# Rebuilding the router stage of a decoder trunk: residual put into the accumulators by identity products, counts in fp32r, an unturned split h, gates computed behind the selection, a first gather over four banks

## The chip, the cores and the metric

One core of one Trainium2 chip runs the whole program. The metric is the device time of one execution in microseconds (us); a kernel is timed in several runs and the median is given. One execution is also recorded by the hardware profiler; its span, from the first to the last recorded instruction, is a little shorter than its device time.

The engines are called PE (TensorE; its weight loads are listed apart as PEld), DVE (VectorE), ACT (ScalarE), POOL (GpSimd) and SP (SyncE, which here only issues transfers).

## The reference, cut to what matters

One layer, 256 tokens, model width 1024, fp32. The change touches the last of its three parts only, the mixture of experts:

```python
x = x + grouped_moe(rms_norm(x, norm_ffn), router_w, router_b, w_gate, w_up, w_down)

logits = h @ router_w + router_b                # 16 experts in 4 groups of 4
probs = softmax(logits)
best = argmax(sum of the two largest of each group)
top_p, top_i = the two largest of that group    # two experts for each token
top_w = top_p / sum(top_p)
out = sum over e of gate_e * ((silu(h @ w_gate[e]) * (h @ w_up[e])) @ w_down[e])
```

Each expert has two matrices of 1024 by 512 and one of 512 by 1024, and all 16 are read from memory.

## The kernel before, in words

Each engine has an instruction stream written out by hand, and the streams meet at semaphores. Before the experts come the mixers and the cross-attention, in which fp32 products are made of fp32r halves (`hi` and `lo`); the change leaves them as they are. Each product is one or more passes on PE, and each pass loads its stationary operand (up to 128 columns, `LDWEIGHTS`) and streams the moving one. An fp32 product is two passes, an fp32r product and a transpose are one.

The output projection of the cross-attention (chunks `C_XO`, `C_XO + 1`) leaves x in `x_res` (128 partitions, two token tiles of 1024), its first 512 columns before its last 512. Then the router:

- PE turns x (L1394), ACT moves it out times a gain (`x2_out`, L756), and PE makes the router logits (`router_products`, L1716). DVE makes `h_full` = x times a gain row, in halves of 512 columns (`h_part`, L1201). ACT reorders it to `h_turn` so that each 128-column tile of h is contiguous (`h_turned`, L778) and rounds it to `h_hi` (L787); DVE makes `h_lo` = `h_turn` - `h_hi` (L1363).
- DVE ranks the experts in a chain of small instructions that ends in `chosen` (L1265), and goes on with the gates (L1266 to L1276). PE makes counts out of `chosen`: five fp32 products with matrices of ones and of a strict triangle (L1747 to L1751). DVE turns them into places (`posm`), the number of rounds and one-hot selections `sel` (`select_tile`, L1290), one instruction for each token tile.
- PE clears the four banks in which the experts' outputs gather by products with zeros (`clear_banks`, L1740): two banks before it waits for `chosen`, two behind the counts.
- `slot_gates` (L1762) brings the gates and the inverse norms of the tokens into slot order; `first_gather` (L1773) then gathers h for the first group of four experts, 8 tiles of 4 passes each. It has two banks: ACT empties the even tiles (L794), DVE the odd ones (L1330), and tile t waits for tile t - 2 to be moved.
- In `expert_round` PE goes through the 16 experts: `gate_up` (L1829, 32 passes of 512 columns), `turn_gate_up`, `down` (L1844, 16 passes), `scatter` (L1864). The gathers for the groups behind the first (24 tiles) stand between these, one bank each. `rounds`, read from memory into a register by every engine ahead of its loop, is 1 here or 2 to 4 for uneven routings; the recorded execution has one round.
- At the end DVE adds the four accumulator banks to `x_res` (L1385), 512 columns each, and SP sends each piece out as it is ready (L485).

SP loads the experts' weights, 96 blocks of 1 MB, into a ring of 16 buffers (`expert_load`, L459); block n waits until PE has used block n - 16 (`mm_done`).

Of the kernel before, what the change touches and what calls it, by code (L numbers as in the profile page):

```python
# [23 lines left out]
P = 128  # L24
S = 256
NT = S // P
D = 1024
# [68 lines left out]
def build_program(nc, d_in, out):  # L96
# [6 lines left out]
    with ctx:  # L103
# [123 lines left out]
        h_hi, h_lo = sb("h_hi", [P, NT, D], f32r), sb("h_lo", [P, NT, D], f32r)  # L227
        h_turn = at("h_turn", xg_at + 8192, [P, NT, D])
# [8 lines left out]
        y_hi, y_lo = sb("y_hi", [P, COLS], f32r), sb("y_lo", [P, COLS], f32r)  # L237
        route = sb("route", [P, 1024])
        router_w = sb("router_w", [P, KD, NE])
        g_ffn_row = sb("g_ffn_row", [P, D])  # L240
        zeros = sb("zeros", [P, P])[:]
# [8 lines left out]
        def sem(name):  # L250
# [32 lines left out]
            out_ready half_rsqrt_ready slot_gates_moved zeros_written x2_rows odd_moved""".split()  # L283
# [128 lines left out]
        def _(sp):  # L412
# [69 lines left out]
            for i in range(NT):  # L482
                for half in range(2):
                    sp.wait_ge(s["out_ready"], 2 * i + half + 1)
                    sp.dma_start(out[0, i * P:(i + 1) * P, half * COLS:(half + 1) * COLS],  # L485
                                 x_res[:, i, half * COLS:(half + 1) * COLS]).then_inc(ld["out"], 16)
# [4 lines left out]
        def _(act):  # L491
# [271 lines left out]

            for i in range(NT):
                x2_square(0, i)
            x2_out(0)
# [9 lines left out]
            def h_turned(n):  # L776
                half = slice(n * P // 2, (n + 1) * P // 2)
                A(h_turn[:].rearrange("q i (t p) -> q i t p", t=KD)[:, :, :, half],  # L778
                  h_full[:].rearrange("q i (p t) -> q i t p", t=KD)[:, :, :, half], ACT.Copy)
# [80 lines left out]
        def _(dve):  # L860
# [332 lines left out]
            V.memset(zeros, 0.0).then_inc(s["zeros_written"], 1)  # L1193
# [10 lines left out]
            h_part(0, 1).then_inc(s["h_full_done"], 1)  # L1204
            dve.wait_ge(mm_done, first_block[C_XO + 2])
# [59 lines left out]
            V.scalar_tensor_tensor(v84(chosen), v84(rank), 2.0, one_group, ALU.is_lt, ALU.mult).then_inc(s["chosen"], 1)  # L1265
            V.tensor_tensor(v84(topw), v84(r2), one_group, ALU.mult)  # L1266
            dve.drain()
            V.reduce_sum(rsum, v2(topw), AX.X)
            dve.drain()
            V.reciprocal(rrec, rsum)  # L1270
            dve.drain()
            V.tensor_tensor(v2(gates), v2(topw), two(rrec, NE), ALU.mult)
            dve.drain()
            V.tensor_copy(gates_split[:, :, 0], v2(gates))
            dve.drain()
            V.tensor_tensor(gates_split[:, :, 1], v2(gates), f32(gates_split[:, :, 0]), ALU.subtract)  # L1276

            dve.wait_ge(s["places_done"], 1)
            V.scalar_tensor_tensor(posm, ps[:, 1, 0:NT * NE], 1.0, chosen, ALU.add, ALU.mult)
# [22 lines left out]
            select_tile(1, slice(0, EPG)).then_inc(s["sel_ready"], 1)  # L1302

            def select(r, g):

                if g:
                    dve.wait_ge(s["sel_turned"], r * (2 * NG) + 2 * g)
                else:
                    dve.wait_ge(s["sel_turned"], r * (2 * NG))
                for i in range(NT):  # L1310
                    V.tensor_copy(gcur[:, i, :, 0:EPG], f32(gates_split[:, i, :, EPG * g:EPG * g + EPG]))
                    ins = select_tile(i, slice(EPG * g, EPG * g + EPG))
                ins.then_inc(s["sel_ready"], 1)
# [13 lines left out]
            def gather_out(r, g, t):  # L1327

                dve.wait_ge(s["gathered"], r * (NG * KD) + (KD * g + t + 1))
                V.tensor_copy(xg[g % 2][:, t].rearrange("p e c -> p (e c)"), ps[:, 1, 0:EPG * SLOTS]).then_inc(s["odd_moved"], 1)  # L1330
# [14 lines left out]
            def expert_round(r):  # L1345
                for e in range(NE):
                    g, j = e // EPG, e % EPG
                    more = g < NG - 1
                    if more and j >= 2:
                        for t in range(4 * j - 8, 4 * j - 4):  # L1350
                            gather_out(r, g + 1, t)
                    if more and j == 1:
                        select(r, g + 1)
# [15 lines left out]
            slot_gates(0, 0)  # L1369
            first_gather_out(0)  # L1370
            dve.wait_ge(s["rounds_ready"], 1)
            rounds = dve.value_load(n_rounds_i[0:1, 0:1], min_val=1, max_val=S // SLOTS)
            with dve.Fori(0, rounds) as r:
                with dve.If(r > 0):
# [3 lines left out]
                    slot_gates(r, 0)  # L1378
                    first_gather_out(r)
                expert_round(r)  # L1380
# [560 lines left out]
```

## Time and profile before

| | |
|---|---|
| device time, median of 3 runs | 626.14 us (624.36 to 628.16) |
| device time of the profiled execution | 624.99 us |
| its span | 623.2 us |
| PE busy | 600.1 us (96%), 2962 instructions |
| PE weight loads busy | 398.1 us (64%) |
| DVE, ACT busy | 275.0 us (44%), 238.0 us (38%) |
| bytes moved | 164.09 MB, mean 263 GB/s |

Busy is the time in which an engine has an instruction in work. Matmuls are pipelined, so a busy PE is not one at its peak: the spacing of the starts of its passes says more than their durations. A row of the timeline gives the start, the time from the first start to the last end, the instruction, and in brackets how long the engine was idle and what ended it.

### The profile page before, as it was taken

What the parts mean: (1) busy time and instruction counts of PE and PEld (TensorE: products, weight loads), DVE (VectorE), ACT (ScalarE), POOL (GpSimd) and SP (SyncE); (2) the same over time, 40 slices, a digit from 0 to 9 for tenths busy, and PEclk for the clock granted to TensorE, in tenths of its full rate; (3) what the DMA queues carried; (4) which work ended last, traced back from release to release, by engine and by line L of the source; (5) the groups of instructions that cost most, each with busy time, mean ns of one, the idle gap of its engine ahead of it and who ended that gap; (6) DMA issues with size and microseconds to landing.
All of it is one profiled execution on the core that took longest, in us unless ns stands there. A gap on an engine that the chain in (4) does not pass through costs nothing.

```text
span 623.2 us, 7542 instructions
## 1 busy us (share of the span) xinstructions
PE 600.1 (96%) x2962; PEld 398.1 (64%) x2962; DVE 275.0 (44%) x414; ACT 238.0 (38%) x318; POOL 19.1 (3%) x13
## 2 busy tenths in 40 slices
PE   4999999999999999999999998999999999999995
PEld 4887888877876777888888788434434434443332
DVE  3734686854577552887665646111102212110002
ACT  5643574654484544734544544311111111111111
POOL 0100000050020000000100100000000000000000
PEclk9999999999999999999999996999999999999999
DMA  9953566854552315756530599699999999999931
GB/s 331 371 204 137 178 228 212 294 202 136 161 155 89 102 69 209 223 176 202 168 103 1 197 426 420 268 418 423 420 421 421 421 421 422 421 420 420 423 155 67
DMA packets 49055, 164.09 MB, mean 263 GB/s; under 512 B 4377, under 2 KB 9179, under 8 KB 36732
## 3 DMA queue, kind: packets, MB, share of 16 engines
q1 hardware_dynamic: 44432, 158.81, 66.1%
q10 hardware_dynamic: 4588, 4.80, 2.4%
q8 instruction: 23, 0.38, 0.2%
q14 instruction: 12, 0.10, 0.0%
HBM read 162.53 MB, written 2.64 MB: 265 GB/s over the span
## 4 chain that ended last, share of the span: by engine, by line
PE 90%; ACT 3%; DVE 3%; issue 1%; DMA 1%; DVEq 1%; SPq 0%; POOL 0%; ACTq 0%
PE ps L1829 18%; PE ps L1421 15%; PE ps L1413 14%; PE ps L1414 14%; PE ps L1844 9%; PE ps L1394 5%; PE ps L1773 3%; PE ps L1864 3%; PE ps L1582 1%; PE ps L1557 1%; DMA w_raw<-in_w_in 1%; ACT w_hi L498 1%; PE ps L1693 1%; PE ps L1716 1%; PE ps L1740 1%
## 5 line engine op out<-in xcount | busy, mean ns | idle before, releaser
L868 DVE TENSOR_TENSOR w_lo<-w_raw,w_hi 128x2048 fp32r<-128x2048 f32 (+2 forms) x54 | 118.4, 2211 | 56.5 <-ACT w_hi L498 55.9
L1413 PE MATMUL ps<-w_hi,act_hi 128*128 128x512 f32 (+1 forms) x304 | 118.7, 392 | 1.8 <-ACT w_hi L498 1.8
L1414 PE MATMUL ps<-w_hi,act_lo 128*128 128x512 f32 (+1 forms) x304 | 116.3, 384 | 0.0
L498 ACT ACTIVATE w_hi<-w_raw 128x2048 fp32r<-128x2048 f32 (+2 forms) x54 | 99.1, 1856 | 26.9 <-PE ps L1421 26.1
L1829 PE MATMUL ps<-e_raw,xg 128*64 128x512 f32 x368 | 82.4, 596 | 0.0
L1421 PE MATMUL ps<-w_lo,act_hi 128*128 128x512 f32 (+1 forms) x304 | 74.2, 386 | 0.0
L1413 PEld LDWEIGHTS ps<-w_hi,act_hi 128*128 128x128 f32 x304 | 57.1, 188 | 14.3 <-issue 3.5
L1414 PEld LDWEIGHTS ps<-w_hi,act_lo 128*128 128x128 f32 x304 | 57.2, 188 | 10.6
L1421 PEld LDWEIGHTS ps<-w_lo,act_hi 128*128 128x128 f32 x304 | 55.6, 188 | 11.5 <-issue 0.7
L1829 PEld LDWEIGHTS ps<-e_raw,xg 128*64 128x64 f32 x368 | 25.1, 137 | 45.6 <-issue 44.0
L807 ACT ACTIVATE gu<-ps,rs_slot 128x512 f32<-128x512 f32 x16 | 11.0, 688 | 111.6 <-PE ps L1829 111.6
L1335 DVE SCALAR_TENSOR_TENSOR y_lo<-ps,w_slot,y_hi 128x512 fp32r<-128x512 f32 x16 | 12.0, 749 | 91.4 <-ACT y_hi L814 91.4
L1844 PE MATMUL ps<-e_raw,a_st 128*64 128x512 f32 x208 | 49.0, 601 | 0.0
L1330 DVE COPY xg<-ps 128x256 f32<-128x256 f32 x28 | 11.9, 425 | 72.9 <-PE ps L1773 72.9
L814 ACT ACTIVATE y_hi<-ps,w_slot 128x512 fp32r<-128x512 f32 x16 | 11.0, 688 | 68.5 <-PE ps L1844 68.5
L1829 PE MATMUL ps<-w_raw,xg 128*64 128x512 f32 x144 | 32.6, 597 | 1.1 <-DVE xg L1330 1.1
L845 POOL TENSOR_TENSOR stat<-stat,const 128x2 f32<-128x2 f32 (+2 forms) x9 | 18.9, 2100 | 353.7 <-DVE stat L895 176.0
L1844 PEld LDWEIGHTS ps<-e_raw,a_st 128*64 128x64 f32 x208 | 13.2, 136 | 23.2 <-issue 22.0
L1829 PEld LDWEIGHTS ps<-w_raw,xg 128*64 128x64 f32 x144 | 10.2, 136 | 18.1 <-issue 17.4
L1773 PEld LDWEIGHTS ps<-sel,h_hi 128*128 128x128 f32 x64 | 9.6, 188 | 19.0 <-issue 18.1
L1413 PE MATMUL ps<-w_hi,mg_hi 128*128 128x512 f32 x48 | 19.2, 400 | 0.0
L1414 PE MATMUL ps<-w_hi,mg_lo 128*128 128x512 f32 x48 | 19.0, 395 | 0.0
(299 smaller groups left out, 723.6 us busy)
## 6 DMA issues: line engine op xcount, KB each, us to landing
w_raw<-in_w_in SPq DMA_DIRECT2D x32, 1024.0 KB, 5.4
e_raw<-in_w_expert_down SPq DMA_DIRECT2D x26, 1024.0 KB, 14.8
e_raw<-in_w_expert_gate SPq DMA_DIRECT2D x23, 1024.0 KB, 14.2
e_raw<-in_w_expert_up SPq DMA_DIRECT2D x23, 1024.0 KB, 15.9
w_raw<-in_w_expert_gate SPq DMA_DIRECT2D x9, 1024.0 KB, 11.1
w_raw<-in_w_expert_up SPq DMA_DIRECT2D x9, 1024.0 KB, 13.5
w_raw<-in_w_expert_down SPq DMA_DIRECT2D x6, 1024.0 KB, 14.0
w_raw<-in_w_xkv SPq DMA_DIRECT2D x4, 1024.0 KB, 5.7
```

Source lines behind the costliest of these rows:

```text
L498: A(bview(w_hi, b, blocks[b].shape), bview(w_raw, b, blocks[b].shape), ACT.Copy).then_inc(hi_done, 1)
L845: nc.gpsimd.tensor_tensor(dst, src, minus_half[:, 0:w], ALU.pow).then_inc(s_rs[n], 1)
L868: V.tensor_tensor(bview(w_lo, b, sh), bview(w_raw, b, sh), f32(bview(w_hi, b, sh)), ALU.subtract).then_inc(lo_done, 1)
L1335: V.scalar_tensor_tensor(y_lo[:], ps[:, 3, :], w_slot[g % 2][:, j:j + 1], f32(y_hi[:]), ALU.mult, ALU.subtract).then_inc(s["y_lo_done"], 1)
L1394: return nc.tensor.transpose(dst, src, ident[0:n, 0:n])
L1413: MM(o, xh[:, t0 + k, i * P:(i + 1) * P], wh[:, k], start=first and k == 0, stop=False)
L1414: MM(o, xl[:, t0 + k, i * P:(i + 1) * P], wh[:, k], start=False, stop=False)
L1421: ins = MM(ps[:, banks + i, 0:width], xh[:, t0 + k, i * P:(i + 1) * P], wl[:, k], start=False, stop=last and k == nt - 1)
L1773: ins = MM(ps[:, bank, 0:EPG * SLOTS], hh[:, i, t * P:(t + 1) * P], sel[:, i, :, 0:SLOTS], start=not k and i == 0, stop=k == 1 and i == NT ...
L1829: ins = MM(ps[side(w), 0, :], xg[g % 2][:, 4 * half + t, j, :], raws[w][:, t * COLS:(t + 1) * COLS], start=half == 0 and t == 0, stop=half ...
L1844: ins = MM(ps[side(w), 3, :], a_st[:, 2 * half + f, :], raw[:, (2 * f + w) * COLS:(2 * f + w + 1) * COLS], start=half == 0 and f == 0, sto ...
L1864: ins = MM(ps[:, 4 + 2 * i + w, :], selT[side(w), j, i * P:(i + 1) * P], y[side(w), :], start=False, stop=False, skip_group_check=True)
```

## The change

- **Accumulators.** The zero products are gone. Instead PE puts x itself into the four banks by fp32 products of the identity with `x_res`, one of 512 columns for each bank: token tile 0 before it waits for `chosen`, tile 1 behind the counts. At the end the banks are only copied out, one half by ACT and one by DVE.
- **Counts.** `chosen` is written in fp32r, and so are the triangle and the ones (`count_w`). Four fp32r products take the place of five fp32 ones.
- **h.** `h_turn` is gone. `h_hi` and `h_lo` have the column order of `h_full` and are made in halves of 512 columns, the first ahead of the second half of x. The gathers read them with a step of 8 elements.
- **Gates.** The arithmetic on the gates stands behind the first gather on DVE, and `slot_gates` of the first group behind the first half of the first expert's gate/up products on PE.
- **Gather.** The first gather goes through banks 0 to 3, and tile t waits for tile t - 4.

```diff
@@ ACT
+            def h_hi_half(n):
+                cs = slice(n * COLS, (n + 1) * COLS)
+                act.wait_ge(s["h_full_done"], n + 1)
+                A(h_hi[:, :, cs], h_full[:, :, cs], ACT.Copy).then_inc(s["h_hi_done"], 1)
             for i in range(NT):
                 x2_square(0, i)
+            h_hi_half(0)
             x2_out(0)
...
             act.drain()
-            act.wait_ge(s["h_full_done"], 2)
-            h_turned(0)
+            h_hi_half(1)
             act.wait_ge(s["router_max_taken"], 1)
             A(prob[:], prob[:], ACT.Exp).then_inc(s["router_exp_done"], 1)
-            h_turned(1)
-            act.drain()
-            A(h_hi[:], h_turn[:], ACT.Copy).then_inc(s["h_hi_done"], 1)
...
-                    A(xg[0][:, t].rearrange("p e c -> p (e c)"), ps[:, 0, 0:EPG * SLOTS], ACT.Copy).then_inc(s["even_moved"], 1)
+                    A(xg[0][:, t].rearrange("p e c -> p (e c)"), ps[:, t % 4, 0:EPG * SLOTS], ACT.Copy).then_inc(s["even_moved"], 1)
...
+            for i in range(NT):
+                act.wait_ge(s["scattered"], rounds * (2 * NE) + i)
+                A(x_res[:, i, 0:COLS], ps[:, 4 + 2 * i, :], ACT.Copy).then_inc(s["out_by_act"], 1)
@@ DVE
             h_part(0, 1).then_inc(s["h_full_done"], 1)
+            def h_lo_half(n):
+                cs = slice(n * COLS, (n + 1) * COLS)
+                dve.wait_ge(s["h_hi_done"], n + 1)
+                V.tensor_tensor(h_lo[:, :, cs], h_full[:, :, cs], f32(h_hi[:, :, cs]), ALU.subtract).then_inc(s["h_lo_done"], 1)
+            h_lo_half(0)
...
-            V.scalar_tensor_tensor(v84(chosen), v84(rank), 2.0, one_group, ALU.is_lt, ALU.mult).then_inc(s["chosen"], 1)
-            V.tensor_tensor(v84(topw), v84(r2), one_group, ALU.mult)
...
+            V.scalar_tensor_tensor(v84(chosen_r[:].rearrange("p i e -> p (i e)")), v84(rank), 2.0, one_group, ALU.is_lt,
+                                   ALU.mult).then_inc(s["chosen"], 1)
+            h_lo_half(1)
...
-            for i in range(NT):
-                V.tensor_copy(gcur[:, i, :, 0:EPG], f32(gates_split[:, i, :, 0:EPG]))
+            select_tile(0, slice(0, EPG))
+            select_tile(1, slice(0, EPG)).then_inc(s["sel_ready"], 1)
             more_rounds(2)
             dve.drain()
-            select_tile(0, slice(0, EPG))
             more_rounds(3)
             dve.drain()
             V.tensor_copy(n_rounds_i[:], total[0:1, 1:2]).then_inc(s["rounds_ready"], 1)
-            select_tile(1, slice(0, EPG)).then_inc(s["sel_ready"], 1)
...
-            dve.wait_ge(s["h_hi_done"], 1)
-            for i in range(NT):
-                ins = V.tensor_tensor(h_lo[:, i, :], h_turn[:, i, :], f32(h_hi[:, i, :]), ALU.subtract)
-            ins.then_inc(s["h_lo_done"], 1)
-            slot_gates(0, 0)
             first_gather_out(0)
+            V.tensor_tensor(v84(topw), v84(r2), one_group, ALU.mult)
...
+            gates_of(0)
...
             for i in range(NT):
                 dve.wait_ge(s["scattered"], rounds * (2 * NE) + i)
-                for half in range(2):
-                    x_ = x_res[:, i, half * COLS:(half + 1) * COLS]
-                    V.tensor_tensor(x_, ps[:, 4 + 2 * i + half, :], x_, ALU.add).then_inc(s["out_ready"], 1)
+                V.tensor_copy(x_res[:, i, COLS:2 * COLS], ps[:, 5 + 2 * i, :]).then_inc(s["out_ready"], 1)
@@ PE
-            pe.wait_ge(s["zeros_written"], 1)
-            clear_banks(range(4, 6))
+            def residual(i):
+                for half in range(2):
+                    MM(ps[:, 4 + 2 * i + half, :], ident[:], x_res[:, i, half * COLS:(half + 1) * COLS], start=True, stop=False,
+                       skip_group_check=True)
+            residual(0)
...
             pe.wait_ge(s["chosen"], 1)
...
-            clear_banks(range(6, 8))
+            MM(ps[:, 1, 0:NT * NE], count_w[:, 0], chosen_r[:].rearrange("p i e -> p (i e)"), start=True, stop=False, skip_group_check=True)
+            MM(ps[:, 1, NE:2 * NE], count_w[:, 1], chosen_r[:, 0], start=False, stop=True, skip_group_check=True)
+            MM(ps[:, 1, 2 * NE:3 * NE], count_w[:, 1], chosen_r[:, 0], start=True, stop=False, skip_group_check=True)
+            MM(ps[:, 1, 2 * NE:3 * NE], count_w[:, 1], chosen_r[:, 1], start=False, stop=True,
+               skip_group_check=True).then_inc(s["places_done"], 1)
+            residual(1)
             pe.drain().then_inc(s["scattered"], 1)
...
             def slot_gates(r, g):
-                pe.wait_ge(s["sel_ready"], r * NG + (g + 1))
+                pe.wait_ge(s["sel_ready"], r * (2 * NG) + (2 * g + 2))
                 if g:
                     pe.wait_ge(s["selT_moved"], r * (2 * NG) + 2 * (g + 1) - 2)
+                else:
+                    pe.wait_ge(s["odd_moved"], r * ODD + 3)
...
-                        ins = MM(ps[:, bank, 0:EPG * SLOTS], hh[:, i, t * P:(t + 1) * P], sel[:, i, :, 0:SLOTS],
+                        ins = MM(ps[:, bank, 0:EPG * SLOTS], hh[:, i, t:D:KD], sel[:, i, :, 0:SLOTS],
...
             def first_gather(r, first=False):
+                pe.wait_ge(s["sel_ready"], r * (2 * NG) + 1)
                 for t in range(KD):
...
+                    if t >= 4:
+                        pe.wait_ge(s["odd_moved"], r * ODD + (t // 2 - 1)) if t % 2 else pe.wait_ge(
+                            s["even_moved"], r * (KD // 2) + (t // 2 - 1))
+                    gather_tile(0, t, t % 4, first)
...
                     gate_up(r, e, 0)
+                    if e == 0:
+                        slot_gates(r, 0)
...
-            slot_gates(0, 0)
             first_gather(0, first=True)
```

In `turn_selection` the first turn of a group now also waits for `slot_gates_moved`, and the first expert's gate/up products wait for three even tiles, and for the fourth only with their second half. For the groups behind the first, `gcur` is filled (`gates_of`) just ahead of the selection, as before, with a semaphore step of its own.

## Rows read from the trace of the kernel before

**Rows 1.** The granted PE clock on the page, 40 slices of the span, tenths of full
```profile
PEclk9999999999999999999999996999999999999999
```

**Rows 2.** PE's own waits from 393 to 617 us: total, times, longest
```profile
PE ps L1829 <- DVE xg L1330: 1.1, 1, 1.1
```

**Rows 3.** Windows: PE, PEld, DVE, ACT, POOL busy; granted clock; DMA share; GB/s
```profile
375.00:376.00 1.00, 1.00 (x9) 1.00 (x8) 0.56 (x4) 0.90 (x3) 0.00 (x0) 0.68 1.04 434
...
385.00:386.00 1.00, 0.92 (x7) 0.66 (x5) 1.00 (x2) 0.00 (x0) 0.00 (x0) 0.70 1.07 451
...
480.00:560.00 80.00, 80.00 (x402) 33.01 (x400) 13.75 (x34) 10.68 (x19) 0.00 (x0) 1.00 1.01 421
```

**Rows 4.** Timeline of DVE from the choice of experts to h_lo
```profile
379.10 0.19 DVE L1265 SCALAR_TENSOR_TENSOR route<-route 128x32 f32<-128x32 f32 x1
...
381.70 0.19 DVE L1279 SCALAR_TENSOR_TENSOR route<-ps,route 128x32 f32<-128x32 f32 x1 [0.66 <-PE ps L1751]
...
382.37 0.24 DVE L1295 CAST gcur<-gates_split 128x8 fp32r<-128x8 f32 x2
...
383.65 0.67 DVE L1290 TENSOR_TENSOR sel<-const,route 128x512 fp32r<-128x512 f32 x1
384.25 2.34 DVE L1363 TENSOR_TENSOR h_lo<-h_turn,h_hi 128x1024 fp32r<-128x1024 f32 x2
```

**Rows 5.** Timeline of PE: counts, cleared banks, slot gates
```profile
379.35 0.61 PE L1747 MATMUL ps<-route,const 128*128 128x16 f32 x2 [1.89 <-DVE route L1265]
...
381.08 0.59 PE L1751 MATMUL ps<-route,const 128*128 128x16 f32 x2
381.50 3.76 PE L1740 MATMUL ps<-zeros 128*128 128x128 f32 x16
385.35 1.16 PE L1762 MATMUL ps<-gcur,sel 128*128 128x10 f32 x8
```

**Rows 6.** Timeline of the first gather and the start of the first expert
```profile
386.36 0.49 PE L1773 MATMUL ps<-sel,h_hi 128*128 128x256 f32 x2
...
390.23 0.40 PE L1773 MATMUL ps<-sel,h_hi 128*128 128x256 f32 x2
390.46 0.40 PE L1773 MATMUL ps<-sel,h_lo 128*128 128x256 f32 x2
...
391.69 0.43 DVE L1330 COPY xg<-ps 128x256 f32<-128x256 f32 x1 [0.84 <-PE ps L1773]
...
392.76 7.09 PE L1829 MATMUL ps<-w_raw,xg 128*64 128x512 f32 x32 [1.11 <-DVE xg L1330]
```

**Rows 7.** Timeline of DVE and ACT around the first and last halves of h
```profile
364.30 1.29 DVE L1201 TENSOR_TENSOR h_full<-x_res,g_ffn_row 128x512 f32<-128x512 f32 x2
...
367.09 1.57 ACT L756 ACTIVATE x2T<-ps,vec_cols 128x256 f32<-128x256 f32 x4 [1.51 <-PE ps L1394]
...
369.39 1.29 DVE L1208 SCALAR_TENSOR_TENSOR x_res<-ps,x_res 128x512 f32<-128x512 f32 x2 [3.80 <-PE ps L1421]
...
377.88 1.91 ACT L787 ACTIVATE h_hi<-h_turn 128x2048 fp32r<-128x2048 f32 x1
```

**Rows 8.** Weight loads by form (busy, mean ns), then two bursts of transposes from the timeline
```profile
L1773 PEld LDWEIGHTS ps<-sel,h_hi 128*128 128x128 f32 x64 | 9.6, 188 | 19.0 <-issue 18.1 <-DVE xg L1330 0.7 <-DVE rs_slot L1325 0.2
...
L1394 PEld LDWEIGHTS ps<-ident,mem_x 128*128 128x128 f32 x16 | 1.9, 193 | 0.1
...
64.08 1.91 PE L1394 MATMUL ps<-ident,zq 128*128 128x128 f32 x16
...
261.58 1.95 PE L1394 MATMUL ps<-ident,mem_x 128*128 128x128 f32 x16
```

**Rows 9.** Timeline of the end
```profile
617.88 2.48 DVE L1385 TENSOR_TENSOR x_res<-ps,x_res 128x512 f32<-128x512 f32 x4 [0.83 <-PE ps L1864]
...
618.60 2.12 SPq L485 DMA_DIRECT2D out<-x_res  x4
```

**Rows 10.** The last four weight blocks, issues from 574 to 604 us, median us to landing
```profile
e_raw<-in_w_expert_down SPq DMA_DIRECT2D x4, 1024.0 KB, 20.3
```

More of the change, by code:

```diff
@@ L226, in build_program @@
         h_full = sb("h_full", [P, NT, D])
-        h_hi, h_lo = sb("h_hi", [P, NT, D], f32r), sb("h_lo", [P, NT, D], f32r)
-        h_turn = at("h_turn", xg_at + 8192, [P, NT, D])
+        h_hi = sb("h_hi", [P, NT, D], f32r)
         sel = sb("sel", [P, NT, EPG, P], f32r)
@@ L483, in _ @@
                 for half in range(2):
-                    sp.wait_ge(s["out_ready"], 2 * i + half + 1)
+                    sp.wait_ge(s["out_ready" if half else "out_by_act"], i + 1)
                     sp.dma_start(out[0, i * P:(i + 1) * P, half * COLS:(half + 1) * COLS],
@@ L1192, in _ @@
             act_lo_part("o", range(2), oT_lo, oT_hi)
-            V.memset(zeros, 0.0).then_inc(s["zeros_written"], 1)
+            V.tensor_copy(count_w[:, 0], before)
+            V.tensor_copy(count_w[:, 1], ones).then_inc(s["count_w_ready"], 1)
             residual_add(C_XO, 0, 1.0)
@@ L1264, in _ @@
             one_group = bc(first.unsqueeze(2), (P, NT * NG, EPG))
-            V.scalar_tensor_tensor(v84(chosen), v84(rank), 2.0, one_group, ALU.is_lt, ALU.mult).then_inc(s["chosen"], 1)
-            V.tensor_tensor(v84(topw), v84(r2), one_group, ALU.mult)
[L1267 to L1276, printed above, removed]
+            V.scalar_tensor_tensor(v84(chosen_r[:].rearrange("p i e -> p (i e)")), v84(rank), 2.0, one_group, ALU.is_lt,
+                                   ALU.mult).then_inc(s["chosen"], 1)
+            h_lo_half(1)
             dve.wait_ge(s["places_done"], 1)
-            V.scalar_tensor_tensor(posm, ps[:, 1, 0:NT * NE], 1.0, chosen, ALU.add, ALU.mult)
+            V.scalar_tensor_tensor(posm, ps[:, 1, 0:NT * NE], 1.0, f32(chosen_r[:].rearrange("p i e -> p (i e)")), ALU.add, ALU.mult)
             V.reduce_max(total[:, 0:1], ps[:, 1, NT * NE:NT * NE + NE], AX.X)
@@ L1301, in _, with gates_of @@
             V.tensor_copy(n_rounds_i[:], total[0:1, 1:2]).then_inc(s["rounds_ready"], 1)
-            select_tile(1, slice(0, EPG)).then_inc(s["sel_ready"], 1)
             def select(r, g):
[L1306 to L1309, printed above, removed]
+                dve.wait_ge(s["sel_turned"], r * (2 * NG) + 2 * g)
                 for i in range(NT):
-                    V.tensor_copy(gcur[:, i, :, 0:EPG], f32(gates_split[:, i, :, EPG * g:EPG * g + EPG]))
                     ins = select_tile(i, slice(EPG * g, EPG * g + EPG))
+                ins.then_inc(s["sel_ready"], 1)
+            def gates_of(g):
+                for i in range(NT):
+                    ins = V.tensor_copy(gcur[:, i, :, 0:EPG], f32(gates_split[:, i, :, EPG * g:EPG * g + EPG]))
                 ins.then_inc(s["sel_ready"], 1)
@@ L1329, in gather_out @@
                 dve.wait_ge(s["gathered"], r * (NG * KD) + (KD * g + t + 1))
-                V.tensor_copy(xg[g % 2][:, t].rearrange("p e c -> p (e c)"), ps[:, 1, 0:EPG * SLOTS]).then_inc(s["odd_moved"], 1)
+                bank = 1 if g else t % 4
+                V.tensor_copy(xg[g % 2][:, t].rearrange("p e c -> p (e c)"), ps[:, bank, 0:EPG * SLOTS]).then_inc(s["odd_moved"], 1)
             def y_lo_part(r, e):
@@ L1367, in first_gather_out @@
                     gather_out(r, 0, t)
-            slot_gates(0, 0)
             first_gather_out(0)
+            V.tensor_tensor(v84(topw), v84(r2), one_group, ALU.mult)
+            dve.drain()
+            V.reduce_sum(rsum, v2(topw), AX.X)
+            dve.drain()
+            V.reciprocal(rrec, rsum)
+            dve.drain()
+            V.tensor_tensor(v2(gates), v2(topw), two(rrec, NE), ALU.mult)
+            dve.drain()
+            V.tensor_copy(gates_split[:, :, 0], v2(gates))
+            dve.drain()
+            V.tensor_tensor(gates_split[:, :, 1], v2(gates), f32(gates_split[:, :, 0]), ALU.subtract)
+            dve.drain()
+            gates_of(0)
             dve.wait_ge(s["rounds_ready"], 1)
@@ L1799, in turn_selection @@
                     pe.wait_ge(s["selT_moved"], r * (2 * NG) + (2 * g + 1))
+                elif not half:
+                    pe.wait_ge(s["slot_gates_moved"], r * NG + (g + 1))
                 for e in (2 * half, 2 * half + 1):
@@ L1821, in gate_up @@
                     else:
-                        pe.wait_ge(s["even_moved"], r * (KD // 2) + KD // 2)
+                        pe.wait_ge(s["even_moved"], r * (KD // 2) + (4 if half else 3))
                         pe.wait_ge(s["odd_moved"], r * ODD + tiles // 2)
@@ L1873, in expert_round @@
                     gate_up(r, e, 0)
+                    if e == 0:
+                        slot_gates(r, 0)
                     if t0 is not None:
@@ L1914, in _ @@
                     pe.wait_ge(s["y_lo_done"], r * NE)
-                    slot_gates(r, 0)
                     first_gather(r)
```

32 lines of the change are left out of this document (7 added, 25 removed).

## The prediction, before the change was run

> **What bounds the kernel now.** I read the page's slices first: the granted PE clock is full in all 40 but the one from 374 to 389 us, the router [rows 1]. Then PE's waits behind the gather: one of 1.1 us, for the last tile of the first gather, and none for weights [rows 2]. Then the windows: from 480 to 560 us PE is busy in all 80.00 us, while the DMA engines are also full at 421 GB/s [rows 3]. So the experts are bound by PE, and what the change can win lies where PE stands still or runs slowly: between the choice of the experts and the first gate/up product, and behind the last product. The timelines of these two stretches are the basis of the sum. Everything behind the choice is one chain: it ends on DVE at 379.29, and the first gate/up pass starts at 392.76 [rows 4, 6]: 13.47 us. All else is a fixed load of PE that moves along with it.
>
> The clock in that stretch: in the slice of one us at 375 it was 0.68, and at 385 0.70 [rows 3]. As only 1.2 and 2.4 GHz occur, it fell at 375.36 and rose at 385.60, thus after 4.1 us of zero products and slot gates without a pause (from 381.50) [rows 5].
>
> **Ahead of the choice: nothing.** The first half of `h_full` is ready at 364.30 + 1.29 = 365.59. ACT has been free since 367.09 - 1.51 = 365.58 [rows 7]. `h_hi_half(0)` rounds 1024 elements; 2048 took 1.91 us [rows 7], so about 1.0: it ends near 366.65, 0.4 us ahead of the turned x that ACT takes next. `h_lo_half(0)` on DVE (1.2 us, half of L1363's two [rows 4]) ends near 367.9; behind it stands the residual sum, which starts at 369.39 at the call of PE [rows 7]. Both are covered; with ACT's cover of 0.4 us gone, x2 and the router's logits would be late by the excess. The second half of `h_hi` (1.0 us) takes the place of a reordering of 2.06 us, ahead of the Exp that DVE waits for. It may cost nothing; a gain is excluded, since the Exp waits for DVE's maximum.
>
> **Counts and places.** Before: ten passes from 379.35, the last starts at 381.08 + 0.22, and DVE begins at 381.70 [rows 4, 5]. Passes start every (381.08 - 379.35) / 8 = 0.216 us at the low clock, whatever their 16 columns. After: four passes, the last starts near 380.0 and ends near 380.4. DVE meanwhile does `h_lo_half(1)` from 379.25: 1.2 us, to 380.45. So `posm` starts at 380.45: **-1.25**. The fp32r form with 16 columns isn't in the trace; were each product still two passes, DVE would start at 381.25 (-0.45); it can't be before 380.45.
>
> **Selection.** Before, from 381.70 to the end of the second `sel` at 383.65 + 0.67 = 384.32: 2.62 us, of which 0.67 up to the casts at 382.37. After: 0.67, then two instructions of 0.69 (0.67 in the row): 2.05, so `sel` is ready at 382.50: **-0.57**. PE puts the second half of x into the banks meanwhile: 2 products, 4 passes of 512 columns, at 1.2 GHz 0.43 each, 380.2 to 381.9. That is hidden by 0.6 us; the passes before `chosen` stand where PE idled for 1.89 us [rows 5].
>
> **Slot gates.** Before, PE came out of the zero products at 385.35, a whole us behind `sel`, and began to gather at 386.36: 2.04 us from `sel` to gather. After: 0.05. The 8 slot gate passes come back behind the first half of the first gate/up: 1.01 us before [rows 5, 6], and a change of tile form besides, say 1.1. Net **-0.89**. The gates' chain on DVE lay between 379.29 and 381.70 [rows 4], so it takes 2.4 us at most, and 0.24 for the casts; from the last tile moved (388.3, below) it ends by 390.9. PE asks for it 3.5 us (16 of the 32 passes in 7.09 [rows 6]) behind the start of gate/up, at 392.3: hidden by 1.4 us. Behind PE's wait stand the second half of gate/up and the turns of `sel`; a chain later than that holds up all of PE.
>
> **Gather.** Before: 386.36 to 392.76, 6.40 us, at full clock almost throughout. Passes start every 0.115 to 0.12 us (390.23, 390.46: two of them), 32 would be 3.8; the rest was waiting for two banks to be emptied and 1.11 us from the last product to the first gate/up, while the copy ended at 392.12 [rows 6]. So 0.64 us of that last gap isn't the copy; it is the read of `rounds`, the entry into the loop, or both. With four banks PE doesn't wait for banks. But it starts at 382.55, when the clock is low. I take its rise at 385.4, near the 385.60 of the trace, since PE is at work again from about the same moment on; then 13 passes take 0.22 each, the other 19 0.119: 5.1, and 0.2 for the last to end: 387.85. The gap up to gate/up I take as 0.95, near the 1.11 seen and less only because the copy needn't be waited for; ends: 0.2 and 1.3. Gate/up starts at 388.8: 6.25 us, **-0.15**. The clock's ends: never low would give 382.55 + 3.8 + 0.2 + 0.95 = 387.5 (1.3 better); low to the end 32 x 0.22 = 7.0, gate/up at 390.75 (1.9 worse).
>
> **A step of 8 elements in the stationary operand,** 128 gather passes, 96 of them among the experts where PE has no slack. The trace has one operand with just this step, `mem_x`: 16 transposes in 1.95 us against 1.91 for contiguous `zq`, so 2.7 ns more for a pass, and its load 193 ns against the 188 that a contiguous gather load takes anyway [rows 8]. 128 x 2.7 ns: **+0.3**. Ends: 0 and 24 tiles x 0.07 (if each tile's first load lies bare) = 1.7.
>
> The Trainium skill (SBUF — State Buffer, the worked part on the DMA port swizzle) says that SBUF has 16-byte lines, and that every access that goes to a new line pays a penalty, so that fp32 is free only up to a step of 4. It gives no size, and the step of 32 bytes is beyond it; by the page the gather loads would lengthen, and the rows show 2.7 ns of it.
>
> **End.** Before, DVE's four sums end at 620.36 and SP issues from 618.60 to 620.72 [rows 9]. After, two pairs of copies of about 0.69 end near 618.6 and 619.3; SP needs about 0.4 for an issue, so it ends near 620.2. But 1 MB of output at the rate of [rows 3] takes 2.5 us from its start, so not all of it counts, and ACT may load a table behind its loop. **-0.3**; ends -0.7 and +0.3.
>
> **Sum:** -1.25 - 0.57 - 0.89 - 0.15 + 0.3 - 0.3 = -2.86. The profiled execution of 624.99 (span 623.2) would be 622.1, and on the median of the three runs, 626.14, the same 2.9 gives **623.2 us**. The loads of weights stay out of it: SP's issues come earlier with PE's first uses, and the DMA idled before 396, so it starts sooner by as much. The last four blocks land 20.3 us after their issue at 574.8 to 579 [rows 10], about 598, while PE uses them from 605 on.
>
> **Rivals.**
> 1. *The clock is hardly low* (or the loop's entry hides behind the gather). For: the identity products have 512 columns where the counts had 16, 1.7 us of them just before the gather. Against: in the trace the clock rose only 4.1 us into zero products of full load [rows 3, 5]. It gives -2.86 - 1.3 = -4.2, with the gap hidden -5.0: 621.1 to 622.
> 2. *The clock stays low through the gather.* For: PE has far less to do from 374.5 to 382.5 than before, 3 us of zero products are gone and those of 3.6 us halved. Against: the gather is as dense as the passes under which it rose. It gives -2.86 + 1.9 = -1.0: 625.2, and a low clock in gate/up besides would take the rest: 626.
> 3. *The stepped loads bind PE* (the other side). The price is paid 128 times; against the 3.2 us that the rest wins it decides from 25 ns a pass. Were the stepped read at half rate, a pass would take 0.218 instead of 0.109 (zq's spacing: 1.91 less the last pass's 0.27, over 15): 128 x 0.109 = +14, 637 us. For: no fp32r operand with a step stands in the trace, and a transpose's contiguous load is shorter than a product's, so `mem_x` may not tell of products. Against: its spacing, 2.7 ns. The page's rule above would be this rival at its full size.
> 4. *The chain isn't shortened at all,* because the gates on DVE or the slot gates hold up the first expert. It needs 1.4 us more than the rows give, and 4 to take the gain: 625 to 626.
>
> **How the numbers follow.** A difference of 0.5% (3.1 us) is about what a measurement of this kernel can tell from none. Chances: the sum as it stands, -1.6 to -4.0, 0.57; rival 1, 0.15; rival 2, 0.14; rival 3, 0.09 (half of it beyond +3.1); rival 4 and a late ACT or DVE ahead of the choice, 0.05. The likeliest is 3.1 us from the bound by a mere 0.2, so its 0.57 divides into 0.26 faster and 0.31 same. Faster: 0.26 + 0.15, and a little of the spread of the runs: 0.43. Slower: 0.045, 0.02, and the spread: 0.09. Same: 0.48. Range: from rival 1 at 620.8 to rival 2 with a cold gate/up and half of rival 4, 626.5.
>
> **What the profile after would show.** `posm`'s first instruction 1.3 us behind the choice instead of 2.4; the gather's first pass 3.3 us behind the choice instead of 7.1; starts of gather passes 0.22 apart, then 0.12 from about 385.5 on; the first gate/up 9.5 behind the choice; slot gates within gate/up without a wait; the loads of `h_hi` at 190 ns and gather tiles among the experts as long as before. I am wrong if those loads are well above 200 ns, if the clock is not back with the gather, or if the table load stands before ACT's last copies on the path.

## The result and the profile after

The changed kernel takes 637.08 us (median of 4 runs, 635.44 to 639.24), the kernel before 625.31 beside it: ratio 1.018, interval 1.014 to 1.021. It is slower by about 11.8 us, outside the range and on the side that the prediction gave 0.09. The profiled execution took 636.96 us, with a span of 635.2.

The page after, busy time and the clock (answers to [rows 1]):

```profile
PE 612.8 (96%) x2932; PEld 407.6 (64%) x2932; DVE 274.3 (43%) x413; ACT 235.3 (37%) x319; POOL 19.3 (3%) x13
...
PEclk9999999999999999999999998999999999999998
```

PE has 30 instructions fewer and is busy 12.7 us longer. The clock is not the reason: up to the last product it is low in one stretch of the router, as before, and for 6.8 us instead of 10.2. So PE has no more passes than before, and some take longer. The groups of weight loads show which (answers to [rows 8]: busy, mean ns):

```profile
L1781 PEld LDWEIGHTS ps<-sel,h_lo 128*128 128x128 f32 x64 | 18.6, 339 | 0.0
L1781 PEld LDWEIGHTS ps<-sel,h_hi 128*128 128x128 f32 x64 | 17.9, 328 | 19.9 <-issue 19.9
...
L1401 PEld LDWEIGHTS ps<-ident,mem_x 128*128 128x128 f32 x16 | 1.9, 193 | 0.1
```

The gather's loads went from 188 to 328 and 339 ns. The transposes of `mem_x`, which have the same step of 8 and on which the prediction priced it, are as they were. The timeline of PE around the second group's gather, among the experts, from the second expert's gate/up on:

```profile
401.29 7.09 PE L1837 MATMUL ps<-e_raw,xg 128*64 128x512 f32 x32
...
416.80 0.75 PE L1781 MATMUL ps<-sel,h_hi 128*128 128x256 f32 x2
417.39 0.64 PE L1781 MATMUL ps<-sel,h_lo 128*128 128x256 f32 x2
417.96 3.65 PE L1837 MATMUL ps<-e_raw,xg 128*64 128x512 f32 x16
```

The same in the kernel before:

```profile
401.31 7.09 PE L1829 MATMUL ps<-e_raw,xg 128*64 128x512 f32 x32
...
416.81 0.51 PE L1773 MATMUL ps<-sel,h_hi 128*128 128x256 f32 x2
...
417.49 3.65 PE L1829 MATMUL ps<-e_raw,xg 128*64 128x512 f32 x16
```

A tile (4 passes) takes 417.96 - 416.80 = 1.16 us from its start to the next work, and 417.49 - 416.81 = 0.68 before. There are 24 such tiles; added up over all of them in the two timelines it is 27.7 us against 15.7, so +12.0, or 0.125 us for each of their 96 passes.

Now the router. The timeline of DVE and PE from the choice of the experts to the first expert (answers to [rows 4, 5, 6]):

```profile
378.50 0.19 DVE L1272 SCALAR_TENSOR_TENSOR chosen_r<-route 128x32 fp32r<-128x32 f32 x1
378.61 1.22 DVE L1209 TENSOR_TENSOR h_lo<-h_full,h_hi 128x1024 fp32r<-128x1024 f32 x1
...
379.46 0.36 PE L1756 MATMUL ps<-chosen_r,count_w 128*128 128x16 f32 x1
379.68 3.76 PE L1746 MATMUL ps<-x_res,ident 128*128 128x512 f32 x4
379.86 0.19 DVE L1277 SCALAR_TENSOR_TENSOR route<-ps,chosen_r 128x32 f32<-128x32 f32 x1
...
380.53 1.29 DVE L1288 TENSOR_TENSOR sel<-const,route 128x512 fp32r<-128x512 f32 x2
...
383.67 0.82 PE L1781 MATMUL ps<-sel,h_hi 128*128 128x256 f32 x2 [0.23 <-issue]
...
391.60 3.65 PE L1837 MATMUL ps<-w_raw,xg 128*64 128x512 f32 x16
395.18 1.05 PE L1770 MATMUL ps<-gcur,sel 128*128 128x10 f32 x8
396.17 3.65 PE L1837 MATMUL ps<-w_raw,xg 128*64 128x512 f32 x16
```

The selection is ready at 380.53 + 1.29 = 381.82, but the gather starts at 383.67: PE is still at the identity products, whose four passes start 0.86 us apart and last to 383.44. The clock in that stretch (windows, columns as in [rows 3]):

```profile
378.00:379.00 1.00, 0.17 (x1) 0.20 (x2) 0.84 (x5) 0.00 (x0) 0.00 (x0) 0.76 1.05 434
385.00:386.00 1.00, 1.00 (x6) 1.00 (x5) 0.10 (x1) 0.39 (x1) 0.00 (x0) 0.82 1.01 426
```

With 1 for the full clock and 0.5 for the low one, it fell at 378.52 and rose at 385.36, 1.7 us into the gather. The end (answers to [rows 9]):

```profile
629.98 1.29 DVE L1392 COPY x_res<-ps 128x512 f32<-128x512 f32 x2 [0.83 <-PE ps L1872]
...
630.60 1.83 SPq L485 DMA_DIRECT2D out<-x_res  x4
```

| part | predicted | measured | how |
|---|---|---|---|
| choice to places | -1.25 | -1.24 | 379.86 - 378.69 = 1.17, before 2.41 |
| selection | -0.57 | -0.66 | 381.82 - 379.86 = 1.96, before 2.62 |
| selection to gather | -1.99 | -0.19 | 383.67 - 381.82 = 1.85, before 2.04 |
| first gather | -0.15 (and part of the step) | +1.53 | 391.60 - 383.67 = 7.93, before 6.40 |
| slot gates within gate/up | +1.1 | +1.14 | first gate/up to the second expert's: 401.29 - 391.60 = 9.69, before 401.31 - 392.76 = 8.55 |
| 24 gathers among the experts | +0.2 of the 0.3 | +12.0 | above |
| end | -0.3 | -0.1 | 635.2 - 629.98 = 5.22, before 5.32 |

The measured column sums to +12.5. From the end of the choice to the end of the span it is 635.2 - 378.69 = 256.5 us, before 623.2 - 379.29 = 243.9: +12.6. The spans differ by 12.0, since in this execution the choice came 0.6 us earlier, out of a part that the change leaves as it is (the half sum of x starts at 362.31, before at 362.92).

### The profile page after: what moved, and what is told of

Read it like the earlier page. It is cut to its first block, busy times and chain, and to the rows that moved or that the text cites. A ratio compares the mean times of both kernels' runs of the same rounds, so it can differ in the third digit from the quotient of the medians.

```text
span 635.2 us, 7493 instructions
## 1 busy us (share of the span) xinstructions
PE 612.8 (96%) x2932; PEld 407.6 (64%) x2932; DVE 274.3 (43%) x413; ACT 235.3 (37%) x319; POOL 19.3 (3%) x13
## 4 chain that ended last, share of the span: by engine, by line
PE 90%; ACT 3%; DVE 3%; issue 1%; DVEq 1%; DMA 1%; POOL 0%; SPq 0%; ACTq 0%
PE ps L1837 18%; PE ps L1428 14%; PE ps L1420 14%; PE ps L1421 14%; PE ps L1852 9%; PE ps L1781 6%; PE ps L1401 5%; PE ps L1872 3%; PE ps L1589 1%; PE ps L1564 1%; ACT w_hi L498 1%; DMA gains<-in_norm_mix 1%; PE ps L1700 1%; PE ps L1723 1%; PE ps L1746 1%
## 5 line engine op out<-in xcount | busy, mean ns | idle before, releaser
L1781 PEld LDWEIGHTS ps<-sel,h_hi 128*128 128x128 f32 x64 | 17.9, 328 | 19.9 <-issue 19.9
L1781 PE MATMUL ps<-sel,h_hi 128*128 128x256 f32 x64 | 23.5, 450 | 0.2 <-issue 0.2
L1781 PE MATMUL ps<-sel,h_lo 128*128 128x256 f32 x64 | 20.7, 405 | 0.0
```

The costliest lines, as they stand in the source:

```text
L1781: ins = MM(ps[:, bank, 0:EPG * SLOTS], hh[:, i, t:D:KD], sel[:, i, :, 0:SLOTS], start=not k and i == 0, stop=k == 1 and i == NT - 1)
```

## The experiments

### Is it the step alone?

The kernels of this section and the next two gather other columns of h than the layer asks for. Their passes and shapes are the same, and they serve only to compare times.

```diff
-                        ins = MM(ps[:, bank, 0:EPG * SLOTS], hh[:, i, t:D:KD], sel[:, i, :, 0:SLOTS],
+                        ins = MM(ps[:, bank, 0:EPG * SLOTS], hh[:, i, t * P:(t + 1) * P], sel[:, i, :, 0:SLOTS],
```

> The changed kernel with one slice undone: the gathers read h in contiguous tiles of 128 columns instead of every 8th column (so they gather h's columns in another order; the number of instructions and their shapes stay). Theory A, the step of 8 in the stationary operand costs 0.12 us in each of 128 passes: the gather's weight loads return from 337 to about 188 ns, a gather tile among the experts from 1.16 to 0.67 us (24 tiles: -11.8), the first gather from 7.9 to 5 to 6 us, so 621 to 623.5 us, below the kernel before. Theory B, the experts run slower for another reason (where h_hi and h_lo now lie, the extra wait of the turns, banks): loads and time stay within 3 us of 637.

The changed kernel with this line: 623.21 us (6 runs), ratio to before 0.992 (0.989 to 0.995). The reverse line in the kernel before:

> The kernel before with that one slice alone: its gathers read every 8th column of the reordered h. Theory A: the weight loads go from 188 to about 337 ns and each of the 128 gather passes costs 0.12 us more: 24 x 0.49 = 11.8 among the experts, and in the first gather up to 3.8 less what the wait for a bank hid (about 1.3 us): +14 to +15.5, 639 to 641 us. Theory B: no change, 625.

640.87 us (4 runs), ratio 1.022 (1.018 to 1.025): +13.5 us at its ratio, just below the 14 to 15.5 expected, which lie within its interval. The group of the `h_lo` loads in the changed kernel with contiguous tiles (busy, mean ns):

```profile
L1781 PEld LDWEIGHTS ps<-sel,h_lo 128*128 128x128 f32 x64 | 10.1, 194 | 0.0
```

The timeline of PE of that kernel, a tile of the second group's gather:

```profile
415.77 0.51 PE L1781 MATMUL ps<-sel,h_hi 128*128 128x256 f32 x2
416.12 0.39 PE L1781 MATMUL ps<-sel,h_lo 128*128 128x256 f32 x2
416.44 3.65 PE L1837 MATMUL ps<-e_raw,xg 128*64 128x512 f32 x16
```

The group of the `h_lo` loads in the kernel before with the step of 8:

```profile
L1773 PEld LDWEIGHTS ps<-sel,h_lo 128*128 128x128 f32 x64 | 18.6, 339 | 0.0
```

One slice moves the loads between 194 and 339 ns and the kernel by about 14 us in either direction (+13.5 above; 637.08 to 623.21 is -13.9), with nothing else changed. Theory B (another place of `h_hi` and `h_lo`, the extra wait of the turns) is out: all of that is in the first kernel, which is faster than the one before. Its first gather shows what the step costs there: 390.57 - 385.39 = 5.18 us up to gate/up, against 7.93 in the changed kernel, so 2.7 us.

### Which step costs?

```diff
-hh[:, i, t:D:KD]
+hh[:, i, t // 4 * 4 * P + t % 4:(t // 4 + 1) * 4 * P:4]      # step 4; with 2 for 4: step 2
```

> The changed kernel with gathers that read every 4th column (16 bytes apart). By a 16-byte line rule in which only an access to a new line pays, a step of 4 fp32 pays just as a step of 8: loads near 337 ns, time 637. If the step of 32 bytes is what costs (or the page's 'free up to 4' holds): loads at 188 ns, 622.

> The changed kernel with gathers that read every 2nd column (8 bytes apart). If what counts is the number of 16-byte lines per column, a load lies between those of steps 1 and 4 or is free (188 ns, 622 us). If any step that isn't 1 falls out of a fast path, 337 ns and 637 us.

One run each: step 4, 636.19 us, loads of 322 and 332 ns; step 2, 624.33 us, loads of 202 and 201 ns. Over the 24 tiles among the experts PE needs 27.1 us at step 4 and 16.2 at step 2, against 27.7 at step 8 and 15.8 at step 1. So 16 bytes already costs nearly as much as 32, and 8 bytes costs next to nothing.

### Which operands, and why did `mem_x` not show it?

Fifteen bursts of 8 small products between the experts, in the kernel with contiguous tiles; they take 26 us (574.3 to 600.5). For instance:

```diff
+                        for t in range(KD):
+                            MM(ps[:, 1, 0:P], hr[:, t:t + 1017:8], one, start=True, stop=True)
...
+                        for t in range(KD):
+                            tr(ps[:, 1, 0:P], hs[:, t:t + 1017:8], ident[:])
```

> The contiguous-slice kernel with 15 bursts of 8 products of 128x128 by 128 columns put into the experts (expert 13), at full clock: fp32r stationary with steps 1, 2, 3, 4, 8; fp32 stationary with 1, 2, 4, 8; transposes with 1, 4, 8; moving operand with 8, 4, 1. If a stepped load costs in any product, fp32 and fp32r alike show loads of about 190 ns at steps 1 and 2 and 330 at 4 and 8, with starts 0.11 and 0.24 apart, and transposes 140, 210, 193 and 0.11 to 0.12. If fp32r alone pays, the fp32 rows stay at 190. Step 3, 1.33 elements a 16-byte line, lies between 2 and 4 if lines are what is counted. A moving operand with a step pays as well if the read itself is slow, and nothing if only the load is.

The trace's answer for each line: duration of the instruction (min/median/max, ns), first and last start. L1890 to L1898 are fp32r at steps 1, 2, 3, 4 and 8; L1904 and L1906 fp32 at 4 and 8; L1908, L1910 and L1912 transposes at 1, 4 and 8; L1914 a product whose moving operand has step 8.

```profile
L1890 PEld LDWEIGHTS ps<-sel,h_hi x8: 186/192/192, 574.3 to 575.1; 128*128 128x128 f32 x8
...
L1892 PEld LDWEIGHTS ps<-sel,h_hi x8: 196/198/200, 575.2 to 576.1; 128*128 128x128 f32 x8
...
L1894 PEld LDWEIGHTS ps<-sel,h_hi x8: 257/262/267, 576.2 to 577.4; 128*128 128x128 f32 x8
...
L1896 PEld LDWEIGHTS ps<-sel,h_hi x8: 320/330/332, 577.6 to 579.2; 128*128 128x128 f32 x8
...
L1898 PEld LDWEIGHTS ps<-sel,h_hi x8: 335/337/337, 579.4 to 581.1; 128*128 128x128 f32 x8
...
L1904 PEld LDWEIGHTS ps<-ident,h_full x16: 313/330/331, 587.6 to 591.1; 128*128 128x128 f32 x16
...
L1906 PEld LDWEIGHTS ps<-ident,h_full x16: 334/335/337, 591.3 to 594.9; 128*128 128x128 f32 x16
...
L1908 PEld LDWEIGHTS ps<-ident,h_full x8: 139/142/269, 595.0 to 595.9; 128*128 128x128 f32 x8
...
L1910 PEld LDWEIGHTS ps<-ident,h_full x8: 198/210/212, 596.0 to 596.8; 128*128 128x128 f32 x8
...
L1912 PEld LDWEIGHTS ps<-ident,h_full x8: 191/194/202, 596.9 to 597.7; 128*128 128x128 f32 x8
...
L1914 PEld LDWEIGHTS ps<-h_hi,sel x8: 192/192/192, 597.9 to 598.6; 128*128 128x128 f32 x8
```

The starts give the spacing: (575.1 - 574.3) / 7 = 0.11 us at step 1, 0.23 at step 4, 0.24 at step 8. The load of a product's stationary operand pays, fp32 and fp32r alike; a transpose hardly does (0.11 to 0.12 us at every step, though its loads lengthen from 142 to 210 and 194 ns); the moving operand doesn't (0.10 to 0.11). The fp32 bursts at steps 1 and 2 can't be read: the clock was low in them, and a contiguous load then takes 333 ns as well. So `mem_x` didn't show the cost because its loads are those of transposes.

The Trainium skill (SBUF — State Buffer, the worked part on the DMA port swizzle) asks for at least two accesses to each 16-byte line. The trace agrees for the stationary operand of a product: steps 1 and 2 have that and are nearly free, step 3 has 1.33 and costs half (262 ns), steps 4 and 8 have one and cost the whole. The same section lets fp32 be read without a penalty up to a step of 4, and there the measurement differs: 330 ns at 4. Why a transpose is nearly spared is open.

### Can the rest of the change be kept?

First the reordering was put back into the instructions that make `h_hi` and `h_lo`:

```diff
-                A(h_hi[:, :, cs], h_full[:, :, cs], ACT.Copy).then_inc(s["h_hi_done"], 1)
+                A(h_hi[:].rearrange("q i (t p) -> q i t p", t=KD)[:, :, :, half],
+                  h_full[:].rearrange("q i (p t) -> q i t p", t=KD)[:, :, :, half], ACT.Copy).then_inc(s["h_hi_done"], 1)
```

and `h_lo` likewise, one instruction for each token tile; the gathers read contiguous tiles. From here on they are the right columns again.

> The changed kernel with h_hi and h_lo again written in turned order (each 128-column tile contiguous), still in halves: the reordering moves into the instructions that make h_hi (ACT, about 2.06 us a half instead of 1.06, by the reordering copy of the kernel before) and h_lo (DVE). Theory A: gather loads at 190 ns and a time within 1.5 us of the contiguous-slice kernel, 622 to 625, ratio to before about 0.992; ACT's extra us is covered behind the second half and costs at most 0.6 ahead of the first turned x. If the reordering itself is what the old kernel paid for, 1 to 2 us more than that.

624.35 us (12 runs), ratio 0.996 (0.994 to 0.998). ACT's part took 2.18 and 2.05 us, as expected. What I hadn't priced is DVE's:

```profile
381.64 0.19 DVE L1277 SCALAR_TENSOR_TENSOR chosen_r<-route 128x32 fp32r<-128x32 f32 x1
381.75 2.06 DVE L1212 TENSOR_TENSOR h_lo<-h_full,h_hi 128x512 fp32r<-128x512 f32 x2
383.73 0.18 DVE L1282 SCALAR_TENSOR_TENSOR route<-ps,chosen_r 128x32 f32<-128x32 f32 x1
...
386.03 0.51 PE L1786 MATMUL ps<-sel,h_hi 128*128 128x256 f32 x2 [1.65 <-DVE sel L1293]
```

Made from a stepped read, in two instructions, `h_lo` takes 2.06 us instead of 1.22, and it stands behind the choice, with the places waiting for it. Two more on top of that kernel: three of the four identity products ahead of the wait for the choice, and then two banks again.

```diff
-            residual(0)
+            residual(0)
+            residual(1, range(1))
...
-            residual(1)
+            residual(1, range(1, 2))
```

> The same, and three of the four identity products ahead of the wait for the choice, one behind the counts. If the gather's start is held by the identity products behind the counts (3.76 us at the low clock, 1.8 us beyond the selection), the gather starts 1.6 to 1.8 us earlier and the time falls by as much (620.5 to 622); if the clock's rise rules instead, it starts earlier but runs longer at the low clock, and half or less of it is left.

> The kernel before this one (turned, identity products early) with the first gather in two banks again: tile t waits for tile t - 2, and the first gate/up for all even tiles. If the four banks save what the old gather waited, each pair of tiles takes 1.26 us instead of 0.95 at full clock: +0.9 to +1.3 us. At a low clock a tile takes 0.88 us and hides the emptying, so with a late rise of the clock +0.3 or less.

623.66 us, ratio 0.997 (0.995 to 0.999), no difference from the 0.996 without it: the 1.6 to 1.8 us expected did not come. The profiled execution of the kernel without it has a reason: there the identity products behind the counts took 1.96 us, at the full clock, and PE then waited 1.65 us for `sel` (last row above), so they held up nothing.

With two banks 625.34 us, ratio 0.999 (0.998 to 1.001). The medians of the two kernels, 12 runs each, differ by 1.7 us and their ratios by 0.0022 (1.4 us), somewhat more than the 0.9 to 1.3 that the banks were expected to be worth, and the intervals just overlap. In the profiled executions the clock was full in the first gather with four banks and low up to 390.2 us in the one with two, so the profiles can't be set against each other for this; the timed runs favour the four banks.

Then the reordering was moved ahead of the choice, to where DVE has idle time, into the product that makes `h_full`:

```diff
+                of = lambda v: v.rearrange("q (p t) -> q t p", t=KD)[:, :, half]
-                return V.tensor_tensor(h_full[:, i, cs], x_res[:, i, cs], g_ffn_row[:, cs], ALU.mult)
+                return V.tensor_tensor(h_full[:, i, :].rearrange("q (t p) -> q t p", t=KD)[:, :, half], of(x_res[:, i, :]),
+                                       of(g_ffn_row[:, :]), ALU.mult)
```

> The changed kernel with the reordering moved into the product that makes h_full (DVE, where it waits for ACT and PE anyway); h_hi and h_lo are then made from contiguous runs of 64 and the gathers read contiguous tiles. The reordering must not stand behind the choice: h_lo of the second half takes 1.2 us there as in the changed kernel, not the 2.06 us of the version with the reordering in h_lo. Expected 622 to 623.5 us (ratio 0.992 to 0.995), 0.8 to 1.5 us below that version. If stepped reads on DVE ahead of the norm's sum delay the logits, it gives 0.5 us back.

622.66 us (7 runs), ratio 0.995 (0.993 to 0.997). It beats both kernels, the one before by a mere 0.5%. The timeline of DVE and PE:

```profile
371.80 1.12 DVE L1204 TENSOR_TENSOR h_full<-x_res,g_ffn_row 128x512 f32<-128x512 f32 x1
...
380.45 0.19 DVE L1277 SCALAR_TENSOR_TENSOR chosen_r<-route 128x32 fp32r<-128x32 f32 x1
380.55 1.22 DVE L1214 TENSOR_TENSOR h_lo<-h_full,h_hi 128x1024 fp32r<-128x1024 f32 x1
...
381.22 1.96 PE L1751 MATMUL ps<-x_res,ident 128*128 128x512 f32 x4
...
382.35 1.29 DVE L1293 TENSOR_TENSOR sel<-const,route 128x512 fp32r<-128x512 f32 x2
...
383.69 0.51 PE L1786 MATMUL ps<-sel,h_hi 128*128 128x256 f32 x2 [0.51 <-DVE sel L1293]
...
388.24 3.65 PE L1842 MATMUL ps<-w_raw,xg 128*64 128x512 f32 x16 [0.51 <-DVE xg L1333]
```

`h_lo` is back at 1.22 us. The reordering isn't free here either: a tile of `h_full` takes 1.12 us instead of 0.69, and from the half sum of x to the choice it is 380.64 - 363.94 = 16.70 us, against 16.38 in the changed kernel. Here the clock was full from the counts on, the identity products took 1.96 us and were covered, and the gather began as soon as `sel` was there: 7.60 us from the choice to gate/up. In the kernel with contiguous slices, with the same stream on PE, the clock was low up to 386.7, and the same way took 390.57 - 380.40 = 10.17. From gate/up on the two agree to 0.05 us (231.66 and 231.63), so the 2.6 us between them lie in the clock of this stretch, the wait for the identity products included.

> The same with three of the four identity products ahead of the wait for the choice. The selection is now ready 1.8 us before the 3.4 to 3.8 us of identity products at the low clock end, so the gather should start 1.5 to 1.8 us earlier than in the run beside it; 620.5 to 622 us (ratio 0.989 to 0.992). If the clock is at full there in most executions (the products then take 1.7 us and are covered), the gain is 0.3 us or less.

622.77 us, ratio 0.995 (0.993 to 0.998): no gain from the early identity products, as the last sentence of its expectation had it; the profiled execution of this kernel too had a full clock at the counts. Last, the counts in fp32:

```diff
-count_w, chosen_r = sb("count_w", [P, 2, P], f32r), sb("chosen_r", [P, NT, NE], f32r)
+count_w, chosen_r = sb("count_w", [P, 2, P]), sb("chosen_r", [P, NT, NE])
```

> The kernel before this one with triangle, ones and choice in fp32: the same four products, eight passes instead of four. h_lo of the second half on DVE (1.2 us) covers the four passes and some more: at the low clock (0.215 us a pass) the counts end 0.5 us behind it, at the full clock (0.11) ahead of it. So +0.3 to +0.6 us or nothing; the 1.25 us that the prediction gave to this part would then belong to the gates' place and the products' number, not to fp32r.

622.09 us, ratio 0.994 (0.992 to 0.996), no slower than the 0.995 beside it. In its trace the clock was full at the counts, and the places begin 1.23 us behind the choice instead of 1.06. The 0.3 to 0.6 us expected at the low clock are less than these intervals can tell.

## Why the prediction was wrong, by its own steps

**The step that failed: "A step of 8 elements in the stationary operand", +0.3.** It measured 0.125 us a pass, not 2.7 ns: 12.0 us in the gathers among the experts and 2.7 in the first, where it turned a gain of 1.2 (5.18 us against the 6.40 before) into the loss of 1.53. The prediction named the place, the number of passes and why there is no slack, and in rival 3 even the size (half rate, +14), but it priced the step by `mem_x`, whose rows are transposes. Its own objection, that a transpose's contiguous load is shorter than a product's (140 against 188 ns), was the sign: the two loads are different, so a row of the one bounds nothing for the other. The upper end of 1.7 us let one load a tile lie bare, where every pass paid, and was no bound. Of the rule of the Trainium skill (SBUF — State Buffer, the worked part on the DMA port swizzle) the prediction said "the rows show 2.7 ns of it"; the rows didn't show the form at all. Its own sign of being wrong, gather loads well above 200 ns, is the one that came: 328 and 339.

**"Counts and places", "Selection": right,** to 0.1 us. What shortened the counts is in part open. In the kernel before, DVE stood idle for 0.66 us until the last count came [rows 4], right behind the gates' arithmetic:

```profile
380.85 0.19 DVE L1276 TENSOR_TENSOR gates_split<-route,gates_split 128x32 fp32r<-128x32 f32 x1 [0.43 <-issue]
```

So with the gates where they were, fewer passes could win those 0.66 of the 1.24 us, and the rest needs the gates moved away; no run takes the two apart. For the form, the last experiment has 0.17 us at the full clock. In the changed kernel the counts ran at the low one and ended at 379.46 + 0.36 = 379.82, just when DVE was free; four more passes, 0.21 us apart, would have come on top, an estimate of 0.8 us that no run shows.

**"Slot gates": of the 1.99 us between selection and gather only 0.19 were won** in the profiled execution, since the identity products behind the counts were put at 1.7 us and took 3.76. A pass of 512 fp32 columns was taken to be 0.43 us at the low clock; it is 0.86 there and 0.43 at the full one. I had divided the 7.09 us of gate/up by its 32 passes, but those have 64 stationary columns each and start in pairs, a pair every 0.43 us. The term is one of the clock: where it was full, the products took 1.96 us and were covered, and three of the four products ahead of the choice instead of two won nothing over 8 and 12 runs. The other part of the term, slot gates within gate/up, was right: 1.14 for 1.1.

**"Gather": the moment of the clock's rise was luck, the gap was too large.** In the changed kernel the clock rose at 385.36 (forecast 385.4). But it had fallen 3.2 us later than before (378.52, before 375.36), which the forecast doesn't have, and the kernel with contiguous tiles, with the same stream on PE, had its rise at 386.7, another no low clock in the gather at all. That PE doesn't wait for banks was right. With contiguous tiles the gather took 5.18 us, not 6.25: six passes at the low clock instead of 13, and 0.59 us from the last product to gate/up instead of 0.95. Gate/up then follows the last copy by 0.13 us (0.06 in the kernel with `h_full` reordered); with two banks it was 0.64 before, and 0.75 in the two-bank version. Whether that is the entry into the loop, which would hide behind the last tiles once PE needn't wait, isn't shown.

**"Ahead of the choice: nothing", and the gates behind the gather: right.** From the half sum of x to the choice it is 378.69 - 362.31 = 16.38 us, before 379.29 - 362.92 = 16.37, and no wait of PE for the slot gates appears.

**"End": -0.3, measured -0.1.** SP's issues shrank from 2.12 to 1.83 us and began 0.1 us sooner behind the first sum or copy, but from the last issue to the end of the span it is 2.77 us instead of 2.48: not all of the gain counts, as was said there.

Without the step, the sum was -3.2 us; the kernel with contiguous tiles measured -0.8% (-0.5 to -1.1), 5 us, and the two versions with `h_full` reordered -0.5% (3.1 us). That the last agrees so well is partly chance: the wait for the identity products and the shorter gather miss in opposite directions. In the profiled executions the stretch from the choice to the end is 2.1 us shorter than before with contiguous tiles, where the clock was low, and 4.7 with `h_full` reordered, where it was full.

## What to carry to other kernels

A step of 16 bytes or more in the stationary operand of a product costs 0.12 us a pass here, at the full clock and with 128 or 256 moving columns; longer passes weren't tried. Before putting one into a loop, look for a row with the same operation, not only with the same step. A reordering belongs into an instruction that waits anyway, and its price on that engine has to be known: on DVE a stepped read made `h_lo` 2.06 us long instead of 1.22. And a price per pass derived from products that run side by side is half of that of one that runs alone.

## What the runs showed of the hardware

- Loads of 128 columns of a product, fp32r: 192, 198, 262, 330, 337 ns at steps of 4, 8, 12, 16, 32 bytes. Transposes: 142, 210, 194 at 4, 16, 32. The odd one is that 16 bytes is worse than 32 for a transpose; why is open.
- The stepped gather had the same spacing at the low and the full clock: in the changed kernel passes start 0.25 us apart at 384.5 and 0.24 at 390, while contiguous ones went from 0.21 at the low clock (385.96 to 386.38, two passes, in the kernel with contiguous tiles) to 0.12. So at the low clock the step costs 0.03 to 0.04 us a pass, not 0.12.
- The clock can fall while PE is busy without a pause. Windows of PE alone in the kernel with the bursts (busy, granted clock, DMA share, GB/s):

```profile
573.00:580.00 7.00, 7.00 (x43) 1.00 1.01 420
581.00:586.00 5.00, 5.00 (x24) 0.50 1.01 421
588.00:595.00 7.00, 7.00 (x32) 1.00 0.84 346
```

It fell at 580.0, in the burst with a step of 8, the last of the fp32r bursts; in the fp32 bursts with steps of 4 and 8 (the last window) it was full again. In the gathers among the experts of the changed kernel, which are stepped too, it stayed full. Why it fell in the one and not in the other no run here tells apart.
